# Second block's residual products with tokens on partitions, operands turned by VectorE

## The reference

```python
def second_block(x, mem, ...):
    h = rmsnorm(x, ln_mix); proj = h @ w_in                       # queries, keys, values, latents
    y_na = neighbourhood_attention(q_na, k_na, v_na, na_rpb)      # 8 heads
    y_mla = latent_attention(c_q, c_kv, k_rope, ...)              # 8 heads
    y = concat([rmsnorm(y_na, na_out_norm), rmsnorm(y_mla, mla_out_norm)])
    x = x + y @ w_out
    h = rmsnorm(x, ln_mem)
    x = x + memory_attention(h, rmsnorm(mem, mem_norm), w_xq, w_xk, w_xv, w_xo)   # 4 heads of 512
    h = rmsnorm(x, ln_ffn)
    x = x + (silu(h @ w_gate) * (h @ w_up)) @ w_down
    return rmsnorm(x, final_norm)
```

## Time and profile before

| what | value |
|---|---|
| span of the profiled execution | 2625.3 us |
| its own time | not given apart; three timed runs are 2628.18, 2625.56, 2628.16 us |
| median of the runs | 2628.16 us, 2.9 us above the span |
| PE busy | 2585.3 us (98%), 14410 products |
| POOL busy | 2190.3 us (83%) |
| DVE busy | 1378.0 us (52%) |
| ACT busy | 1237.4 us (47%) |
| DMA | 224 GB/s over the span |

### The profile page before, as it was taken

One profiled execution on the slowest core, in us unless ns is written; L12 is line 12 of the kernel. 1 busy time (PEld: TensorE's weight loads), 2 busy tenths in 40 slices (PEclk: granted clock), 3 DMA queues, 4 the chain that ended last, 5 costly groups with the idle time before them and its releaser, 6 DMA issues.

```text
span 2625.3 us, 39163 instructions
## 1 busy us (share of the span) xinstructions
PE 2585.3 (98%) x14410; PEld 2260.4 (86%) x14410; DVE 1378.0 (52%) x2103; ACT 1237.4 (47%) x1522; POOL 2190.3 (83%) x889
## 2 busy tenths in 40 slices
PE   8999999999999999999999999999999999999998
PEld 8989999897888888888898888989888888888886
DVE  6767767576888888622466247722332222223223
ACT  5445465544444444445663454534544444444444
POOL 7888866778999999898999755866888888889996
PEclk9999999999999999999999999999999999999999
DMA  9998987665666665455455543634555555555553
GB/s 389 412 393 334 415 344 295 212 230 186 239 242 242 241 240 192 176 191 183 172 191 209 178 141 129 241 130 158 187 191 195 193 194 193 192 192 192 192 192 128
DMA packets 101758, 587.34 MB, mean 224 GB/s; under 512 B 11240, under 2 KB 13416, under 8 KB 45200
## 3 DMA queue, kind: packets, MB, share of 16 engines
q1 hardware_dynamic: 93600, 570.07, 58.9%
q10 hardware_dynamic: 8048, 15.74, 1.8%
HBM read 579.46 MB, written 8.40 MB: 224 GB/s over the span
## 4 chain that ended last, share of the span: by engine, by line
PE 74%; POOL 15%; issue 9%; DVE 2%; ACT 0%; POOLq 0%; DVEq 0%; ACTq 0%
PE ps L1365 15%; PE ps L1373 15%; PE ps L1367 15%; POOL w_lo L557 15%; PE ps L1325 6%; PE ps L1342 6%; PE ps L1330 3%; PE ps L1347 3%; PE ps L1285 2%; PE ps L1292 2%; PE ps L1287 2%; PE ps L1980 1%; PE ps L1955 1%; PE ps L1644 0%; PE ps L1444 0%
## 5 line engine op out<-in xcount | busy, mean ns | idle before, releaser
L557 POOL TENSOR_TENSOR w_lo<-raw,w_hi 128x1024 fp32r<-128x1024 f32 x884 | 2189.9, 2491 | 417.0 <-ACT w_hi L580 412.0
L580 ACT CAST w_hi<-raw 128x1024 fp32r<-128x1024 f32 x884 | 926.3, 1052 | 1129.9 <-PE ps L1373 689.2
L1365 PE MATMUL ps<-w_hi,a_both 128*128 128x512 f32 x1976 | 773.9, 392 | 0.0
L1367 PE MATMUL ps<-w_hi,a_both 128*128 128x512 f32 x1976 | 769.2, 389 | 0.0
L1373 PE MATMUL ps<-w_lo,a_both 128*128 128x512 f32 x1976 | 528.4, 389 | 0.0
L1373 PEld LDWEIGHTS ps<-w_lo,a_both 128*128 128x128 f32 x1976 | 371.0, 188 | 77.0
L1365 PEld LDWEIGHTS ps<-w_hi,a_both 128*128 128x128 f32 x1976 | 371.1, 188 | 76.7
L1367 PEld LDWEIGHTS ps<-w_hi,a_both 128*128 128x128 f32 x1976 | 371.1, 188 | 76.0
L1285 PE MATMUL ps<-a_both,w_hi 128*128 128x256 f32 x1488 | 372.1, 288 | 8.0 <-issue 3.3
L1287 PE MATMUL ps<-a_both,w_hi 128*128 128x256 f32 x1488 | 366.1, 284 | 0.0
L1285 PEld LDWEIGHTS ps<-a_both,w_hi 128*128 128x128 f32 x1488 | 286.2, 192 | 11.5 <-issue 4.2
(11 more groups left out here) (279 smaller groups left out, 2167.6 us busy)
## 6 DMA issues: line engine op xcount, KB each, us to landing
raw<-stream SPq DMA_DIRECT2D x440, 1024.0 KB, 4.8
arena<-ada SPq DMA_DIRECT2D x182, 512.0 KB, 7.7
work<-ada SPq DMA_DIRECT2D x10, 512.0 KB, 7.5
arena<-memT SPq DMA_DIRECT2D x4, 512.0 KB, 9.9
res<-xT SPq DMA_DIRECT2D x4, 512.0 KB, 11.6
v_spill<-arena ACTq DMA_DIRECT2D x4, 512.0 KB, 4.6
k_spill<-arena ACTq DMA_DIRECT2D x4, 512.0 KB, 6.7
rel_rows<-rel_row ACTq DMA_DIRECT2D x4, 512.0 KB
```

The costliest lines, as they stand in the source:

```text
L557: pool.tensor_tensor(w_lo[:, h % SLOTS], raw_half(h), w_hi[:, h % SLOTS].bitcast(F32), ALU.subtract).then_inc(lo_ready, 1)
L580: act.copy(w_hi[:, base % 4], raw[:, tile_slot, (base % 2) * HALF:(base % 2 + 1) * HALF]).then_inc(hi_ready, 1)
L1365: pe.matmul(out2[:, t, :], a_hi[:, c0 + k, a], w_hi[:, h % SLOTS, w], start=first and k == 0, stop=False, skip_group_check=True)
L1367: pe.matmul(out2[:, t, :], a_lo[:, c0 + k, a], w_hi[:, h % SLOTS, w], start=False, stop=False, skip_group_check=True)
```

## The change

- The 128 halves of the second block that were `half_T` or `half_pair` with queries, keys, output, cross query and cross output become `half_N`. `half_pair` goes, and with it the special order of those weights in the stream.
- The residual is turned by PE once, in `win2` instead of in `gu`; ACT copies it out of PSUM with the token's factor as its scale. Four DVE products of `res` by a row (L2777) go. From there on `res` has tokens on partitions, and the output products add to it with one scaled add per token tile (`out_residual`).
- Query and key groups are copied to a staging area by ACT with the token's factor (`stage_out`), and DVE turns them with 16 block transposes (`stage_turned`).
- For the norms before `xq` and `gu`, DVE turns each quarter of `res` (`quad_in`, 16 block transposes), ACT makes the high part with the gain (`turned_high`), DVE the low part in four instructions (`turned_low`). The squares are summed by ACT per token (`squares`), and the roots are made over 128x2 values, all in SBUF (`token_norm`, `token_factors`). The `row_sums` of these two norms go; those of `na` and `mla` become `token_sums` of one column.
- Four order changes: `scores_x` stands 4 halves into a group and not 2, `turn_x` 7 and not 5, `values_x` follows one half into the next group; the first two groups of `xo` are interleaved by halves (`XO_HALVES`).

```diff
+            def turned(src, dst):
+                for a in range(4):
+                    for b in range(4):
+                        x = src[32 * a:32 * a + 32].rearrange("p t (c n) -> p c t n", c=4)
+                        y = dst[32 * b:32 * b + 32].rearrange("p c (t n) -> p c t n", t=2)
+                        ins = dve.transpose(y[:, :, :, 32 * a:32 * a + 32], x[:, :, :, 32 * b:32 * b + 32])
+                return ins
+            def stage_turned(k, G, dst):
+                dve.wait_ge(evac[G % 2], G // 2 + 1)
+                turned(staging(k), dst).then_inc(staged_turned, 1)
+            def quad_in(name, q):
+                if q >= 2:
+                    dve.wait_ge(al_ready, al_before(name) + q - 1)
+                turned(res_tok(q), tmp_of(q)).then_inc(quad_turned, 1)
+            def turned_low(name, q):
+                dve.wait_ge(ah_ready, al_before(name) + q + 1)
+                for j in range(4):
+                    c = 4 * q + j
+                    ins = dve.scalar_tensor_tensor(out=a_lo[:, c, :], in0=tmp_of(q)[:, j, :], scalar=col(name + "_g", c),
+                                                   in1=a_hi[:, c, :].bitcast(F32), op0=ALU.mult, op1=ALU.subtract)
+                ins.then_inc(al_ready, 1)
...
+            def token_factors(name):
+                root(tok_v, tok_u, TOKENS[name])
...
-            mix_out("wb2", 0, row_b)
-            mix_out("wb2", 1, row_b)
-            low_of_ring("lnmem", 0, 0)
-            add_up(K0["lnmem"], part(0))
-            mix_pair("wb2", 2, 0, row_b)
...
+            for q in range(4):
+                mix_out("wb2", q, "mla")
+                if q == 3:
+                    turned_low("lnmem", 2)
+                quad_in("lnmem", q)
+                if q in (1, 2):
+                    turned_low("lnmem", q - 1)
+            turned_low("lnmem", 3)
+            token_norm("lnmem", 8)
...
+            xo_out(0)
+            quad_in("lnffn", 0)
+            xo_out(1)
+            quad_in("lnffn", 1)
+            xo_out(2)
+            turned_low("lnffn", 0)
+            quad_in("lnffn", 2)
+            turned_low("lnffn", 1)
+            xo_out(3)
+            turned_low("lnffn", 2)
+            quad_in("lnffn", 3)
+            turned_low("lnffn", 3)
+            token_norm("lnffn", 16)
```

ACT's new order at the two norms, and PE's in the cross attention:

```diff
+            squares("lnmem", 2, "wb2")
+            his(hb2 + 17, 3)
+            turned_high("lnmem", 2, hx)
+            squares("lnmem", 3, "wb2")
+            his(hx + 4, 3)
+            turned_high("lnmem", 3, hx)
...
+                stage_out(4 + x, G0["xq"] + x, hx + 8 * x + 8, lambda t: token("lnmem", t))
...
+            his(hg, 2)
+            turned_high("lnffn", 2, ho + 30)
             his(hg + 2, 2)
+            squares("lnffn", 3, "xo")
+            his(hg + 4, 3)
+            turned_high("lnffn", 3, ho + 32)
...
+            for n in range(40):
+                if n % 8 == 4 and n < 32:
+                    scores_x(24 + n // 8)
+                if n % 8 == 7 and n < 32:
+                    turn_x(24 + n // 8)
+                if n % 8 == 1 and n > 8:
+                    values_x(23 + n // 8)
```

More of the change, by code:

```diff
@@ L887, in wait @@
                     else:
[L888 to L890 removed]
+                        G = G0[name] + q
+                        act.wait_ge(evac[G % 2], G // 2 + 1)
                 return wait
@@ L1084, in _, with squares, turned_high, upto @@
                    .then_inc(reload_done, 16)
-            def operand_of(name, q, from_, free, gain):
+            def squares(name, q, from_):
                 residual_ready(from_)(q)
[L1089 to L1105, removed]
+                for t in range(2):
+                    before = (8 if name == "lnffn" else 0) + 2 * q + t - 1
+                    if before > 0:
+                        act.wait_ge(tsq_ready, before)
+                    act.activation(scratch[:, 512 * t:512 * t + 512], res_tok(q)[:, t, :], ACT.Square,
+                                   accum_out=token_squares(name)[:, 4 * t + q:4 * t + q + 1]).then_inc(tsq_ready, 1)
+            def turned_high(name, q, free):
+                act.wait_ge(quad_turned, (4 if name == "lnffn" else 0) + q + 1)
+                act.wait_ge(half_used, free)
+                gained(a_hi[:, 4 * q:4 * q + 4, :], tmp_of(q), lambda j: col(name + "_g", 4 * q + j)).then_inc(ah_ready, 1)
+            his(hb2 + 7, 2)
+            squares("lnmem", 0, "wb2")
+            his(hb2 + 9, 3)
+            turned_high("lnmem", 0, hb2)
+            his(hb2 + 12, 1)
+            squares("lnmem", 1, "wb2")
+            his(hb2 + 13, 2)
+            turned_high("lnmem", 1, hb2)
+            his(hb2 + 15, 2)
+            squares("lnmem", 2, "wb2")
[4 more added lines that the diff above has]
+            turned_high("lnmem", 3, hx)
+            cast = [hx + 7]
+            def upto(p):
+                his(cast[0], hx + 9 + p - cast[0])
+                cast[0] = hx + 9 + p
             def exp_x(u):
@@ L1143, in _ @@
[L1143 to L1152, removed]
@@ L2032, in _ @@
+            for n in range(16, 32):
+                xo_half(n)
+            for n in range(16):
+                half_of("N", "gu", n, al=al_before("lnffn") if n < 8 else None)
             groups("N", "gu", 2, 22)
-            pe.wait_ge(rt_copied, 4)
             down("down2", 22)
@@ L2913, in _ @@
-            add_up(K0["lnmem"] + 1, part(1))
-            mix_pair("wb2", 3, 0, row_b)
-            mix_pair("wb2", 3, 1, row_b)
-            low_of_ring("lnmem", 2, 8)
-            low_of_ring("lnmem", 3, 12)
-            add_up(K0["lnmem"] + 2, part(2))
-            add_up(K0["lnmem"] + 3, part(3))
-            parts_ready(25)
-            means("lnmem", (v1, D))
-            root(v1, u1, row_c)
+            dve.wait_ge(r_summed, NORM["mla"])
+            link(dve.tensor_scalar(tok_v, ps[:, 5, 0:2], 1.0 / 1024, EPS, ALU.mult, ALU.add))
@@ L3094 @@
 DOWN_ORDER = [0, 2, 4, 1, 3, 5] + list(range(6, 44))
-def _in_pairs(w, first=0, last=None):
-    w = [w[:, 512 * g:512 * g + 512] for g in range(w.shape[1] // 512)]
-    last = len(w) if last is None else last
-    return np.concatenate([_tiles(c, 256, 8) if first <= g < last else _tiles(c) for g, c in enumerate(w)])
 def _down_tiles(w):
```

432 lines of the change are left out of this document (177 added, 255 removed).

## The result

The changed kernel takes 2637.34 us (median of 5 runs, 2633.71 to 2638.11), the kernel before, in as many, 2628.16 (2625.56 to 2630.78). The ratio is 1.0032, with a 95% interval of 1.0022 to 1.0043: slower by 0.32%. The forecast was 2634.4 us. The profiled execution took 2633.71 us with a span of 2631.9.

A forecast was written before the change was run, and what follows sets the result against it. PE's own instructions were taken to bound the kernel: 2625.3 - 16.9 + (3.1 + 4.4 + 4.3) + 11.3 = 2631.5 us of span, with the median 2.9 us above it, 2634.4 us, 0.24% slower. The range was 2610 to 2647 us.

The forecast's parts named there:

- the signs named: What a profile should show: turned_low mean 1 to 2 us, PE idle about 7 us at xq, 11 at gu, 4 before cross scores.
- PE's instructions: Second block: cheaper halves, dropped row sums and less missed time beside the heads take 16.9 us off PE.
- Transposes: DVE's 16 block transposes per turned quad or group, 32x256 within SBUF: about 0.45 us each, 7.2 us for 16.
- 7 to 8 as a mean with POOL at work: Norms before xq and gu: a turned_low group of four waits for POOL's instructions, 7 to 8 us, bounds 2 and 10.
- choice of the row over the rule: At each norm POOL loses 2 us, hidden by its idle time, as measured; the skill's rule would give 8 us.
- The first gaps: PE stalls for turned_low: 3.1 and 4.4 us at xq, 4.6 and 6.7 us at gu.
- The stall at the first scores: After xq's norm, PE waits 4.3 us for the root, scaled copies and transposes before the first cross scores.
- stalls of 23.1 us at full clock: PE's waits at both norms: 3.1, 4.4 and 4.3 us around xq, 11.3 us at gu.
- Without stalls: Rival: turned_low costs 2 us everywhere, so PE never waits at xq or gu; 2611.3 us, chance 0.26.
- The condition named for that: At the norm before xq: turned_low(0) under 3 us would decide for the case of 2611.3 us.
- Roots that all wait: Rival: before the first scores each of 12 small root instructions waits for a whole POOL instruction; 2651 us, chance 0.09.
- POOL's pace: Rival: POOL at 2.40 us sets the pace, so PE's halves don't shorten; 11.8 us less gain, 2646 us, chance 0.07.

The follow-up runs named there:

- psum_root: psum_low with the two token norms' sums and roots also given operands in PSUM (bank 5); 2610.77 us, ratio 0.9936 to the kernel before.
- psum_low: Changed kernel with the norms' turned quads written to PSUM, so turned_low reads one SBUF operand, not two; 2616.9 us, ratio 0.9956 to the kernel before.
- one_low: Changed kernel with turned_low as one instruction per quad instead of four, ACT rounding in a second pass; 2620.85 us, ratio 0.9976 to the kernel before.
- fill: Changed kernel with additional unused PE products in the four gaps at xq and gu; 2635.25 us, ratio 1.0024 to the kernel before.
- quarter_turn: Changed kernel with 4 of 16 block transposes per norm quad, so wrong operands; 2616.17 us, ratio 0.9957 to the kernel before.
- eight_low: Changed kernel with turned_low in eight instructions of 128 columns per quad, not four of 256; 2650.97 us, ratio 1.0087 to the kernel before.

## Why the prediction was right

The sign and the mechanism held; the size came out by a sum in which one term was missing and another did not come. Of the signs named, the mean of a `turned_low` instruction was 1.35 us (1 to 2 predicted), and PE idled 7.2 us at `xq` (about 7) and 7.8 at `gu` (11), each time for `turned_low`, but nothing before the first scores (4).

- **PE's instructions: 16.9 us predicted, 16.3 measured.** psum_root has the changed kernel's PE instructions and no stall from 1645 us on; its span is 2609.0 against 2625.3. In the windows of 590 to 605 and 1075 to 1090 us psum_root and the kernel before have the same granted clock, 0.89, so the difference is no clock loss of the first block.
- **Transposes: 7.2 us for 16 predicted, 7.18 measured** (436 ns each). `out_residual` 1.5 predicted, 1.41 measured.
- **`turned_low`: 2 us with POOL idle predicted, 1.67 measured; 7 to 8 as a mean with POOL at work, 6.54, 10.07 and 10.25 measured**. Two groups took 1.67; three took 3.66, 3.76 and 3.76, in each of which one of the four met a POOL instruction (2.48 to 2.57 us) and the others took 0.47 to 0.48. On the rule of the Trainium skill, "SBUF — State Buffer", section "Who interferes with whom": DVE's wait agrees, and psum_low shows that it is the second SBUF operand that makes it. The three POOL instructions wholly beside the group of 10.25 us took 2.57 to 2.58 us each, those of psum_low in that stretch 2.41 to 2.44, so POOL loses some 0.17 us for each and not the 0.48 of DVE's instruction. The prediction's choice of the row over the rule stands.
- **The first gaps.** Predicted for the end of `turned_low(1)` 1686.7, measured 1686.47; for `turned_low(3)` 1700.3 to 1702.8, measured 1702.14. The first gap was 4.34 us, not 3.1, because PE asked 1.4 us sooner. The other three came shorter than predicted, 2.89 for 4.4, 2.49 for 4.6, 5.32 for 6.7: the second and the fourth mostly because PE reached them 1.7 us late with half its clock, the third because DVE needed 26.8 us from the start of `turned_low(0)` to the end of `turned_low(2)` and not 28.9.
- **The stall at the first scores (4.3 us) did not come.** Only three of the 13 small instructions waited, the root ended at 1710.84 and not 1714, and PE came 2 us later, 1.7 of them its own lost clock. psum_low, one_low and fill show it, with 3.73, 4.97 and 2.94 us: it is real, and was hidden by the other gaps and the clock behind them.
- **The clock was missing from the sum.** Predicted: stalls of 23.1 us at full clock. Measured: gaps of 15.0 us and 7.4 us of half clock behind them, 22.4 together; the spans say 2631.9 - 2609.0 = 22.9. The total agrees by chance. The absent stall and the shorter gaps (8.1 us less) stand against the clock (7.4 us more).
- **The rivals.** Without stalls the prediction gave 2611.3 us: psum_root took 2610.77. The condition named for that, `turned_low(0)` under 3 us, is what psum_low set. Roots that all wait did not come in this kernel, though four or five of 13 waited in psum_low, one_low and fill. POOL's pace is out: N halves lie 2.72 us apart (1678.40 to 1681.12).

Open: the changed kernel's other four timed executions have spans of 2635.3 to 2636.3 us, 3.4 to 4.4 above the profiled one. The sum forecast a span of 2631.5 us and the profiled one is 2631.9; the median lies 5.4 us above that span and not 2.9, so the forecast time is 2.9 us short for a reason that the sum does not hold. More instructions that met POOL, or one more stretch of half clock, would do it; no trace of them exists. The clock does differ between executions of unchanged work: between 590 and 605 us, in the first block, it is 0.89 in the kernel before, the changed kernel and psum_root, and 0.77 in psum_low, one_low, fill and quarter_turn, which is 15 x 0.12 = 1.8 us.

## What to carry to other kernels

A chain of small VectorE instructions must be priced by what GpSimd does beside it: with both inputs in SBUF (for the 128x2 ones even with one) each can take a whole GpSimd instruction, and the cure is an operand in PSUM, or fewer and longer instructions. A gap of TensorE as long as the four here (2.49 to 5.32 us) should be charged with the lower clock behind it too, here 1.7 to 2.3 us, unless a later wait covers it. When a fix removes the waits that end last, look for the one they hid: here it was the root, worth another 6 us.

## What was not expected of the hardware

- From `wb2` on, the granted clock was at half behind every gap of 2.49 us or more (2.49, 2.89, 2.90, 2.94, 3.73, 4.34, 4.97, 5.32 us, and the four of eight_low, 5.33 to 9.29) and behind none of 0.45 to 1.61 us. This is no fixed border. In the first block, all runs have a gap of 3.00 us near 1083 us: behind it the clock fell in the kernel before (0.55 from 1082.53 to 1086.00 us), but in one_low (1082.67 to 1086.00) and in quarter_turn (1083.15 to 1087.00) it stayed at 1.00. And in fill it fell behind a gap of 1.84 us (0.60 from 360.70 to 365.00 us). In the changed kernel and in psum_low the lower clock behind one gap cost 1.7 to 2.8 us beside the gap. The first row is the window behind 3.73 us in psum_low, (1 - 0.53) x 5.89 = 2.8 us; the second that behind 1.61 us in quarter_turn:

```profile
1714.11:1720.00 5.89, 5.89 (x15) 4.78 (x16) 0.00 (x0) 0.00 (x0) 3.06 (x2) 0.53 0.69 241
```

```profile
1902.00:1908.00 6.00, 5.82 (x26) 4.82 (x27) 4.15 (x14) 1.05 (x1) 3.96 (x2) 1.00 0.58 220
```

- A DVE instruction of 128x2 elements with a single input, in SBUF, a scaling or a shift, waited for POOL as the large ones do, 2.16 and 2.29 us, and took 0.17 us with input and output in PSUM. The Trainium skill, "SBUF — State Buffer", section "Who interferes with whom", names `tensor_scalar` among the operations that can take the ports shared with GpSimd, on conditions for its operands; these rows agree, and show it at two elements a partition. Not every such instruction waits: the sum just before them, also with a single input in SBUF, took 0.15 us while a POOL instruction ran from 1701.82 to 1704.38 us:

```profile
1702.06 0.15 DVE L2245 TENSOR_REDUCE small<-mod 128x2 f32<-128x8 f32 x1
1702.25 2.16 DVE L2247 TENSOR_SCALAR small<-small 128x2 f32<-128x2 f32 x1
1704.44 2.29 DVE L2146 TENSOR_SCALAR small<-small 128x2 int32<-128x2 int32 x1
```
